# A gather-and-weigh kernel: every eighth row of the weighted sum taken off TensorE, gate rows kept in PSUM

## The reference, cut to what matters

```python
mix = jnp.concatenate([y_a, y_b, y_c], axis=-1) @ w_out[l]
x = x + g_m[:, None] * mix
h = _rmsnorm(x, norm_ffn_g[l]) * (1.0 + sc_f[:, None]) + sh_f[:, None]
# peer_ffn, for a chunk of 128 tokens:
u = jnp.take(u_tab, eidx, axis=0)
act = jnp.einsum('thkd,td->thk', u, hc)
coef = gate * jax.nn.gelu(act, approximate=False)
vsel = jnp.take(v_tab, eidx, axis=0)
y = jnp.einsum('thk,thkd->td', coef, vsel)
x = x + g_f[:, None] * y
```

## Time and profile before

| | us |
|---|---|
| median of 3 runs | 1902.0 (1898.29 to 1904.04) |
| profiled execution | 1903.03 |
| its span | 1901.2 |
| PE, DVE, ACT, POOL busy | 1616.6, 1394.7, 673.4, 515.2 |

### The profile page before, as it was taken

One profiled execution on the slowest core, in us unless ns is written; L12 is line 12 of the kernel. 1 busy time (PEld: TensorE's weight loads), 2 busy tenths in 40 slices (PEclk: granted clock), 3 DMA queues, 4 the chain that ended last, 5 costly groups with the idle time before them and its releaser, 6 DMA issues.

```text
span 1901.2 us, 20926 instructions
## 1 busy us (share of the span) xinstructions
PE 1616.6 (85%) x6868; PEld 1006.0 (53%) x6868; DVE 1394.7 (73%) x3315; ACT 673.4 (35%) x1640; POOL 515.2 (27%) x564
## 2 busy tenths in 40 slices
PE   1767678898999998898999998898999997887776
PEld 1656665554665655564665655554665652332222
DVE  5866598997856758998765748988765759985554
ACT  1313114334732334335632235325632233331112
POOL 2000013222233232222233232222232233343331
PEclk9889788998999999998999999999999998999999
DMA  9982688997799999998999999998899999999996
GB/s 393 422 346 101 242 353 348 367 421 286 283 399 421 422 420 395 363 422 313 321 403 421 421 421 399 370 402 293 287 403 421 421 415 401 416 407 421 421 421 256
DMA packets 96989, 706.08 MB, mean 371 GB/s; under 512 B 10992, under 2 KB 11504, under 8 KB 13296
## 3 DMA queue, kind: packets, MB, share of 16 engines
q0 software_dynamic: 80640, 587.24, 77.1%
q1 hardware_dynamic: 16240, 117.50, 15.1%
HBM read 703.64 MB, written 1.05 MB: 371 GB/s over the span
## 4 chain that ended last, share of the span: by engine, by line
PE 49%; DVE 28%; DMA 16%; ACT 3%; issue 3%; POOL 0%; DVEq 0%; ACTq 0%; POOLq 0%
PE psum L772 26%; DMA ringmem<-in_peer_uv_dram,eidx 11%; DVE ringmem L1435 9%; PE psum L648 5%; PE psum L412 4%; DMA W<-in_w_groups_dram 3%; PE psum L635 2%; DMA ringmem<-in_ada_pairs_dram 2%; PE psum L520 1%; PE psum L508 1%; DVE ringmem L1079 1%; PE psum L518 1%; PE psum L415 1%; DVE coef L1448 1%; ACT diag L1050 1%
## 5 line engine op out<-in xcount | busy, mean ns | idle before, releaser
L772 PE MATMUL psum<-ringmem,diag 128*128 128x512 f32 x2048 | 978.4, 624 | 132.3 <-ACT diag L1050 132.0
L379 POOL DMA_INDIRECT ringmem<-in_peer_uv_dram,eidx x512 | 489.5, 956 | 1131.5 <-PE psum L772 1079.7
L1435 DVE SCALAR_TENSOR_TENSOR ringmem<-ringmem,psum 128x1024 f32<-128x1024 f32 x512 | 612.5, 1220 | 195.3 <-DMA ringmem<-in_peer_uv_dram,eidx 180.1
L772 PEld LDWEIGHTS psum<-ringmem,diag 128*128 128x128 f32 x2048 | 389.1, 199 | 608.1 <-issue 409.1
L1050 ACT ACTIVATE diag<-K,coef 128x128 f32<-128x128 f32 x512 | 176.4, 393 | 225.8 <-DVE coef L1448 225.6
L412 PE MATMUL psum<-hT,W 128*128 128x128 f32 x1344 | 172.3, 287 | 40.9 <-DMA W<-in_w_groups_dram 19.1
L412 PEld LDWEIGHTS psum<-hT,W 128*128 128x128 f32 x1344 | 169.2, 203 | 64.9 <-issue 38.0
L1042 ACT ACTIVATE coef<-dots 128x2 f32<-128x2 f32 x256 | 51.8, 202 | 408.6 <-DVE ringmem L1435 407.7
L1079 DVE SCALAR_TENSOR_TENSOR ringmem<-ringmem,diag 128x1024 f32<-128x1024 f32 x96 | 115.3, 1223 | 20.9 <-DMA ringmem<-in_ada_pairs_dram 18.8
L648 PEld LDWEIGHTS psum<-hT,W 128*128 128x128 f32 x1024 | 123.2, 197 | 12.8 <-issue 7.2
L648 PE MATMUL psum<-hT,W 128*128 128x128 f32 x1024 | 126.0, 281 | 3.1 <-ACT hT L821 3.0
(11 more groups left out here) (243 smaller groups left out, 1629.7 us busy)
## 6 DMA issues: line engine op xcount, KB each, us to landing
ringmem<-in_ada_pairs_dram POOLq DMA_DIRECT2D x48, 1024.0 KB, 19.0
W<-in_w_pieces_dram SPq DMA_DIRECT2D x48, 1024.0 KB, 9.2
W<-in_w_groups_dram SPq DMA_DIRECT2D x24, 1536.0 KB, 11.3
W<-in_w_groups_dram SPq DMA_DIRECT2D x12, 1024.0 KB, 9.6
ringmem<-in_peer_uv_dram,eidx POOLq DMA_INDIRECT x512, 11.7
W<-in_w_groups_dram SPq DMA_DIRECT2D x4, 1040.0 KB, 9.2
attn<-in_subkeys_t_dram SPq DMA_DIRECT2D x4, 1024.0 KB, 9.5
K<-in_consts_dram SPq DMA_DIRECT2D x1, 1546.0 KB, 18.1
```

Of the source, the lines that this page charges most:

```text
L379: nc.gpsimd.indirect_dma_start(slot(k), None, rows, bass.IndirectOffsetOnAxis(ap=eidx[:, ph % 2, m:m + 1], axis=0)).then_inc(row_landed[q ...
L772: mm = nc.tensor.matmul(acc[:, q], diag[:, k % DIAGS, :], slot(k)[:, D:][:, q], start=(k % SEL == 0), stop=(k % SEL == SEL - 1), skip_grou ...
L1435: ins = v.scalar_tensor_tensor(out=u, in0=u, scalar=1.0, in1=hrep, op0=ALU.mult, op1=ALU.mult, accum_out=dots[:, j:j + 1])
```

## The change

Rows with k % 8 == 5 (16 a phase, 64 in all; the second row of every fourth tick) are no longer weighed by TensorE. ScalarE scales v by the row's coefficient, and GpSimd adds it to a sum in SBUF, `accv`. The first such row of a phase needs no add: ScalarE writes it scaled into `accv`. The others are scaled in place. GpSimd's add stands in its queue right before the gather that reuses the slot, and frees the slot. `add_sum` first adds `accv` to `acc`, then multiplies by the gate row. `grow` and the gate copies are gone: eight diagonals are written into the buffer `tm`, one call of `gate_row` fills two PSUM banks, and VectorE reads them there. The mixing gate is built later (diagonals in segments 50 and 51, matmuls behind the second output product in segment 52), the PEER gate in segments 75 to 77.

```diff
+        def on_gpsimd(k):
+            return k % 8 == 5
...
+                def weigh(k):
+                    pool.wait_ge(s["v_weighed"], k // 8 - k // SEL)
+                    nc.gpsimd.tensor_tensor(accv[:], accv[:], slot(k)[:, D:], ALU.add).then_inc(freed(k)[0], 1)
+                    pool.wait_ge(*freed(k))
+
                 for k in range(PHASES * SEL):
+                    if k >= RING and on_gpsimd(k - RING) and (k - RING) % SEL != 5:
+                        weigh(k - RING)
...
-                            pe.wait_ge(s["g_sb"], g_at(i, 0))
                             pe.wait_ge(s["q_sb"], at("q_sb", i, 0))
+                        if i > 1:
+                            pe.wait_ge(s["x_done"], i - 1)
...
                             out_product(seg - 51)
+                            if seg == 52:
+                                gate_row(g_at(i, 0), 4)
...
+                def gate_row(nth, b):
                     pe.wait_ge(s["g_diag"], nth + 1)
+                    for k in range(KD):
+                        mm = nc.tensor.matmul(bank[b + k // 4][:, k % 4 * P:(k % 4 + 1) * P], ones[:], gdiag[:, k, :],
+                                              start=True, stop=True)
                     mm.then_inc(s["g_out"], 1)
...
                     for k in range(n * BATCH, (n + 1) * BATCH):
+                        if on_gpsimd(k):
+                            continue
...
                     for k in range(n * BATCH, (n + 1) * BATCH):
                         j = k % (NBUF * BATCH)
+                        if on_gpsimd(k):
+                            if k % SEL == 5:
+                                if k >= SEL:
+                                    act.wait_ge(s["sums_taken"], k // SEL)
+                                w = nc.scalar.activation(accv[:], slot(k)[:, D:], ACT.Copy, scale=coef[:, j:j + 1])
+                                w.then_inc(freed(k)[0], 1)
+                            else:
+                                nc.scalar.activation(slot(k)[:, D:], slot(k)[:, D:], ACT.Copy, scale=coef[:, j:j + 1]
+                                                     ).then_inc(s["v_weighed"], 1)
+                            continue
                         ins = nc.scalar.activation(diag[:, k % DIAGS, :], ident, ACT.Copy, scale=coef[:, j:j + 1])
...
-                        dve.wait_ge(s["g_sb"], g_at(i, half + 1))
-                        step(v.tensor_tensor(hm[:, q], bank[6 + half][:, :], grow[:, q], ALU.mult), "wo_taken")
+                        dve.wait_ge(s["g_out"], g_at(i, 1))
+                        step(v.tensor_copy(hm[:, q], bank[4 + half][:, :]))
+                        step(v.tensor_tensor(hm[:, q], bank[6 + half][:, :], hm[:, q], ALU.mult), "wo_taken")
...
-                    step(v.tensor_tensor(hm[:], acc, grow[:], ALU.mult), "sums_taken")
+                    dve.wait_ge(*freed((ph + 1) * SEL - 3))
+                    step(v.tensor_tensor(hm[:], acc, accv[:], ALU.add), "sums_taken")
+                    dve.wait_ge(s["g_out"], g_at(ph + 1, 2) if ph + 1 < PHASES else g_at(PHASES, 1))
+                    step(v.tensor_tensor(hm[:], psum[:, 6 * 512:8 * 512], hm[:], ALU.mult))
```

More of the change, by code:

```diff
@@ L193, in trunk @@
         stat = sb("stat", [P, 8])
-        grow = sb("grow", [P, D])
+        accv = sb("accv", [P, D])
         ringmem = sb("ringmem", [P, RING, 2 * D])
@@ L381, in _ @@
                                                  ).then_inc(row_landed[q % RING], 16)
+                for k in range(PHASES * SEL - RING, PHASES * SEL):
+                    if on_gpsimd(k):
+                        weigh(k)
             @block.tensor
@@ L737, in mixing @@
                             query(*divmod(seg - QRY0, 2))
-                        if i and seg == 75:
-                            gate_row(g_at(i, 2), gdiag[1], bank[6], ("q_sb", at("q_sb", i, 7)))
-                        elif i and seg == 76:
-                            gate_row(g_at(i, 3), gdiag[1], bank[6], ("g_sb", g_at(i, 3)))
-                def gate_row(nth, src, dst, bank_free):
+                        if i and seg == 77:
+                            pe.wait_ge(s["q_sb"], at("q_sb", i, PH))
+                            gate_row(g_at(i, 1), 6)
+                def gate_row(nth, b):
                     pe.wait_ge(s["g_diag"], nth + 1)
-                    pe.wait_ge(s[bank_free[0]], bank_free[1])
-                    for j in range(4):
-                        mm = nc.tensor.matmul(dst[:, j * P:(j + 1) * P], ones[:], src[:, j, :], start=True, stop=True)
+                    for k in range(KD):
+                        mm = nc.tensor.matmul(bank[b + k // 4][:, k % 4 * P:(k % 4 + 1) * P], ones[:], gdiag[:, k, :],
+                                              start=True, stop=True)
                     mm.then_inc(s["g_out"], 1)
                 def last_gate():
-                    for n in range(2):
-                        yield 75 + n
-                        gate_row(g_at(PHASES, n), gdiag[1], bank[6],
-                                 ("g_sb", g_at(PHASES, n)) if n else ("q_sb", at("q_sb", PHASES, 0)))
+                    yield 77
+                    pe.wait_ge(s["x_done"], PHASES - 1)
+                    gate_row(g_at(PHASES, 0), 6)
                 def place_h(ph):
@@ L791, in gate_exp, with gate_diag @@
                     nc.scalar.activation(e, e, exp, accum_out=gsum[:, i % 2, h:h + 1]).then_inc(s["gate_exp"], 1)
-                def gate_diag(l, section, half, dst):
-                    for j in range(4):
-                        ins = nc.scalar.activation(dst[:, j, :], ident, ACT.Copy,
-                                                   scale=MC[:, l, section, 4 * half + j:4 * half + j + 1])
-                    ins.then_inc(s["g_diag"], 1)
-                def gate_copy(nth, half, src):
-                    act.wait_ge(s["g_out"], nth + 1)
-                    nc.scalar.activation(grow[:, half * 512:(half + 1) * 512], src, ACT.Copy).then_inc(s["g_sb"], 1)
+                def gate_diag(l, section, half):
+                    for k in range(4 * half, 4 * half + 4):
+                        ins = nc.scalar.activation(gdiag[:, k, :], ident, ACT.Copy, scale=MC[:, l, section, k:k + 1])
+                    if half:
+                        ins.then_inc(s["g_diag"], 1)
                 def mixing(i):
```

51 lines of the change are left out of this document (23 added, 28 removed).

## The result

| | us |
|---|---|
| before, median of 4 runs beside it | 1901.3 (1898.3 to 1904.0) |
| changed kernel, median of 4 runs | 1935.0 (1931.0 to 1938.6) |
| ratio | 1.0177, 95% interval 1.0151 to 1.0204 |
| its profiled execution, and the span | 1931.02, 1929.2 |

I had forecast 1891.

A forecast was written before the change was run, and what follows sets the result against it. Gathers at the 421 GB/s ceiling bound full stretches; less TensorE work helps only where TensorE leads. Terms -16.0 - 6.0 + 6 + 0.7 + 3.7 - 0.1 + 1 = -10.7 took 1903.03 to 1892.3, 1891 on the median; range 1876 to 1916.

The forecast's parts named there:

- TensorE's weighing, -22.0: Rows off TensorE: -16.0 us at ticks 26, 30, 34 and -6.0 at tick 18 of three phases; elsewhere 0.
- Rival A: After a short tick the chain through mask, exponential and diagonals leads, taking back half of 16 us: 1899, chance 0.27.
- "Does the add hold up VectorE?", +6: In each phase's first 24 ticks, ten of 20 adds matter, costing half of 12 us: +6 us.
- Rival B: GpSimd's adds stop VectorE: all 20 early adds count at 1.7 us, +34, giving 1919 on the median; chance 0.18.
- the number that would overturn the sum: Threshold for adds holding VectorE: more than 0.8 us of VectorE's time lost per add.
- The gate rows, +0.7: Lead-in: moved gate matmuls cancel at 1.16 us, a PSUM copy adds 0.69: +0.7 us; in the phases 0.
- The third operation, +3.7: Phase-end sum gets a third 1024-wide VectorE operation, 1.224 us at the start of phases 1 to 3: +3.7 us.
- GpSimd's queue, 0: Adds queued before the gathers that reuse slots: later issue is taken up in full stretches, 0 us.
- rival C: GpSimd's queue becomes the bound if an add with all belonging to it exceeds 12.3 us: about 1993, chance 0.03.
- ScalarE's scalings, 0: Each removed row costs ScalarE 0.75 us more, behind the other row's diagonal; diagonals have 3.2 us to spare: 0.
- TensorE's clock in ticks with one row, +1: Longer pauses may start the next weighing at 1.2 GHz, 1.7 us longer; 0 to 25 us, taken as +1.
- The tail, -0.1: At the very end the last pair finishes 1.35 us sooner, against 1.22 for the third operation: -0.1 us.

The follow-up runs named there:

- e2: Changed kernel with GpSimd's 60 adds left out, ScalarE scaling as before and freeing the slots itself: 1892.8 us, ratio 0.9936 to the kernel before.
- e1: Changed kernel's gate rows alone: all 128 rows of a phase weighed by TensorE, a copy replacing the first sum add: 1915.0 us, ratio 1.0061.
- e11: Kernel before with seven rows a phase in phases 0 to 2 scaled by ScalarE instead of weighed, their 18 GpSimd adds left out: 1878.2 us, ratio 0.9872.
- e5: Changed kernel with rows k % 8 == 1 taken off TensorE in place of k % 8 == 5: 1933.9 us, ratio 1.0160 to the kernel before.
- e3: Changed kernel with each GpSimd add replaced by a memset of the same slot half: 1895.7 us, ratio 0.9957 to the kernel before.
- e6: e1 with eight more matmul records on constants at each of two places in the lead-in: 1907.9 us, ratio 1.0044 to the kernel before.

## Why the prediction was wrong, step by step
**TensorE's weighing, -22.0: right in the sum, in part by luck.** e2 against e1 gives -22.2. By the table above the phases bring -9.2, -5.9 and -8.9 at their last rows, and phase 3 gives 1.6 back. The TensorE-led stretch did what the prediction says: from tick 24 to tick 40 e2 gains 4.5, 5.0 and 5.7 us on e1, 15.2 against 16.0. But up to tick 24 it gains 7.5, -0.9 and 4.9, 11.5 us where I had 6.0 for tick 18, in one step between ticks 20 and 21 of phases 0 and 2, and in phase 1 none; why, no run shows. And some 4 us are given back behind tick 40 and in phase 3, where I had 0. Two misses cancel. Rival A, the gain taken back on the way, did not come: it needed the chain through ScalarE to lead; in e2 VectorE waited less for ScalarE than before (29.8 us against 41.1). With seven rows a part was given back (e11).

**"Does the add hold up VectorE?", +6: the step that failed; it measured +42.** I named the mechanism and mis-sized it three times over.
- The length. "Half of the near end", 1.22 us an add, came from VectorE's own add; GpSimd's took 2.356. The Trainium skill (GPSIMD Engine Reference, section 3.1) had led me to estimate 2.25, and I had let the sum "stand as it is" by that.
- Which operations are held. I looked at L1150 and L1152 and argued that `row`, with one operand in PSUM, is spared. It is: 13 of its operations began during an add and none was longer. But all 14 coefficient operations that began so were held, and 10 that began just before, though two elements wide. That operation is in every tick, on the way from GELU to diagonal to weighing. A short operation waits as long as a long one, up to the add's end. The Trainium skill (SBUF — State Buffer, "Who interferes with whom") states that a VectorE instruction with two SBUF inputs clashes with a GpSimd instruction that reads SBUF, not with one that only writes it; that copy, cast and tensor_scalar can run in modes with two ports and then clash with GpSimd as well; and that the one that waits is blocked for the whole instruction. These traces agree: 3.01 us for the coefficient operation, 1.73 for the cast in e5, 692 ns unchanged beside the memsets of e3, and the tensor_scalar held by memsets there. In which mode an operation ran, no trace shows. I had cited the rule and counted it at 10 us, because I applied it to two lines of the kernel instead of to every VectorE line with its operands.
- How many adds count. I took ten of twenty. All of the first 24 ticks count, at 1.4 to 1.7 us, and those behind them at 0.2 or less. Phase 3, which has no mixing, alone lost 11 us to them by tick 24, five adds at nearly their full length. I had seen VectorE's 91% in phase 0, and had no row of phase 3's first 25 ticks.

Rival B priced the same mechanism at 20 x 1.7 = 34 us. By the table the 20 early adds cost 34.3 us, so B had the place, the sign and the size. The size was luck in part: its 1.7 us was half of an add of 3.4 us, and what came is an add of 2.36 that held an operation in 16 cases of 20, for 2.1 us each. "More than 0.8 us of VectorE lost per add" was the number that would overturn the sum; it was 1.28 (77 us over 60 adds).

**The gate rows, +0.7: wrong, 6.5 to 8.** I added up matmuls and copies and let the clock be. The gate matmuls at 193 and 196.87 us were what TensorE had to do right before the next heavy work; without them the granted clock of 200 to 225 us was 0.50 instead of 0.73, its lower level all through. e6 brought it back to 0.80 with idle matmuls. In the text I had looked at the clock only for ticks with one row.

**The third operation, +3.7: right** (1.5, 1.3 and 1.3 us in e1). At tick 2 of phase 3 e1 is 1.3 late, e2 2.5 and the changed kernel 3.3. The wait for GpSimd's last row, which I had put at 0, can be in the last 0.8 alone, since e2 has no adds; no run separates the rest.

**GpSimd's queue, 0: right.** e3 bounds it at 3 us, and the rate is 421 GB/s from 555 to 729 us. The 415 GB/s from 1725 us on is under the 420 that I had named as a sign of rival C, but it is the late start of the full stretch, as said above. Rival C is ruled out. **ScalarE's scalings, 0: right** as a whole, since e2 has them all; 1.135 us each, forecast 1.148.

**TensorE's clock in ticks with one row, +1: not disproved.** From 1725 to 1885 us the granted clock is 0.87 instead of 1.00, and the rate from 1755 us on is still 421 to 422. From tick 24 to the last row phase 3 takes 192.1 us in the changed kernel and 190.6 before: 1.5.

**The tail, -0.1: right in its parts.** The last pieces of the chain of the changed kernel, which answer to the earlier trace rows:

```profile
1913.51 0.70 ACT diag L1071 x2
...
1914.25 3.71 PE psum L789 x8
...
1918.05 1.24 DVE hm L1478
...
1919.31 1.24 DVE hm L1480
```

The last pair is weighed in 3.7 us as soon as its diagonals are there, and the added operation takes 1.24.

Together: 1902 + 12.5 (e1) - 22.2 (e2 against e1) + 42.2 (the adds) = 1934.5, against 1935.0 measured. That this closes proves nothing, since each term is the difference between one kernel and the next; it says how large each is. Against the sum of the prediction the adds are 36 us off (42.2 for 6) and gate rows and third operation together 8 (12.5 for 4.4).

## What to carry to other kernels
Before work is put on GpSimd, list every VectorE operation by where its operands lie: a GpSimd instruction that reads SBUF stopped those with two inputs in SBUF, and some with one, until it was done, and of the smallest of them, on the way to the next matmul, most were held. Price it by place: the held time in full where VectorE leads, little where a transfer does. And where a change takes matmuls away ahead of a dense stretch, read the granted clock of the stretch behind them, since the work left there may run at half speed.

## What the runs showed of the hardware
- VectorE's operation of 0.22 us took 3.01 beside a GpSimd add of 2.36, and a `row` with an operand in PSUM 1.22 as ever.
- In the changed kernel the hold set in up to 0.65 us before the add's recorded start and ended 0.03 us behind it (24 coefficient operations).
- Back to back, four GpSimd pieces of 0.73 us kept a VectorE addition of 0.69 us out for all four (3.29 us), but let the coefficient operation in between two pieces (0.80 us at most). Cutting up the add helped only 6 of 42 us.
- A memset on GpSimd (0.965 us for 128x1024) delayed no VectorE operation with two inputs, but a tensor_scalar of 0.17 us took up to 1.62; a copy (1.042 us) delayed both.
- One-input operations of VectorE that write SBUF from SBUF were held too: the 128x32 conversion in e5 (1.73 for 0.18 us, once 2.98). The searches (MAX8, FIND_INDEX8, MATCH_REPLACE8) were not, in 15 cases that began during an add of the changed kernel.
- 8 matmuls on constants in the lead-in raised the granted clock of 200 to 225 us from 0.53 to 0.80 and ended the program 7 us sooner.
